# A mixture-of-experts loop: transposes moved from TensorE to VectorE, with the row layout and the weight loads that this needs

## The chip, the cores and the metric

The kernel runs on one core of one Trainium2 chip. The metric is the device time of one execution in microseconds (us), the median of three runs. Below, PE is TensorE, PEld its weight loads, DVE VectorE, ACT ScalarE, POOL GpSimd, and SP the sync engine, which here only issues DMAs. All data is float32.

## The reference

One decoder block on 512 tokens of width 1024. A gated delta-rule group and a convolution group share an input and an output projection; then each token goes to 4 of 32 experts, and a final norm follows. What matters here is the expert part:

```
xn = rmsnorm(x, ffn_norm_w)
gates, experts = softmax(top4(xn @ w_router + b_router))
for each expert e, for its tokens:
    hid = xn @ w_gate_up[e] + b_gate_up[e]            # 1024 -> 2048
    gate, up = hid[:, :1024], hid[:, 1024:]
    act = (clip(up, -7, 7) + 1) * min(gate, 7) * sigmoid(1.702 * min(gate, 7))
    y[tokens] += gates * (act @ w_down[e] + b_down[e])  # 1024 -> 1024
out = rmsnorm(x + y, final_norm_w)
```

The weights of one expert are 8 MiB (gate and up) and 4 MiB (down), read from HBM once; over 32 experts that is 403 MB. 512 tokens with 4 experts each make 2048 pairs of a token and an expert, 64 to an expert on average.

## The kernel before, in words

Up to about 430 us the kernel does the two mixer groups, the output projection, the norm and the routing. Then comes the expert loop, one visit for each expert, which takes the rest but for the last 28 us.

**Tokens.** A visit has up to four groups of 32 tokens. Groups 0 and 1 are always worked on, 2 and 3 only where an expert has more than 64 or 96 tokens; unused slots of a group are pads, which point at spare rows behind the 512 real ones. The normed rows (`xn_rows`) and the sums (`acc_rows`) lie in DRAM, seen as four quarter rows of 256 elements to a row. POOL gathers with one indirect DMA a group: partition 32j+s gets quarter j of the row of slot s, 128 pieces of 1 KB. The results go back with an indirect DMA that adds into `acc_rows`, also 128 pieces of 1 KB.

**Gathered rows to the stationary operand.** A matmul wants the contracted index on the partitions. So PE turns the gathered tile (`xt_turn`, line L1808, 8 transposes of 128x128 a visit), and ACT copies it from PSUM (`xT_copy`, L849 and L850).

**gate_up(i)** (L1836). For each of 8 chunks of 128 contracted rows (1 MiB of weights, a slot of `ring`) and each group, four matmuls, one for each quarter of the output columns; they go to the four 32-partition quarters of bank g. In float32 each stands twice in the profile. In the middle of it 16 small matmuls (L1797) work out the row numbers of a later visit.

**hid_turn and act_part.** ACT copies the four banks to SBUF (`hid_copy`, L858). PE turns them (`hid_turn`, L1904, 8 transposes for the gate half, 8 for the up half). DVE adds the bias straight from PSUM (L1410, L1417) and clamps, ACT makes the sigmoid, DVE multiplies (L1424, L1429).

**down(i-1)** (L1878). Four units of 1 MiB (`dslots`), 8 matmuls for each group and unit. ACT scales the result with the gates (L866), POOL scatters it.

**Order.** Every engine's order is written out by hand. On PE a pass of the loop is gate_up(i), xt_turn, down(i-1) units 0 and 1, hid_turn of the gate half, units 2 and 3, hid_turn of the up half. SP issues, in this order, the 8 gate_up transfers of the next visit, each once PE is done with that slot, and the 4 down transfers, each once PE is done with that unit. So weights are at most about one visit ahead. All DMAs, those of POOL too, run on the same 16 DMA engines.

Elsewhere the change touches the norm ahead of the router (`normed`, L1218, DVE; POOL then writes the rows to DRAM, L525), and the turning of the biases early in the kernel (`bias_turn`, L1485).

Of the kernel before, what the change touches and what calls it, by code (L numbers as in the profile page):

```python
# [22 lines left out]
ALU = mybir.AluOpType  # L23
ACT = mybir.ActivationFunctionType
AX_X = mybir.AxisListType.X

P = 128
# [11 lines left out]
def block_kernel(nc, x, attn_norm_w, w_in, gdn_conv_w, gdn_a_log, gdn_dt_bias, gdn_norm_w, cf_dw_w, cf_dw_b,  # L39
# [30 lines left out]
    with ExitStack() as ctx:  # L70
# [48 lines left out]
        bgu_rows = wq[0:E, 0:2 * D]  # L119
# [41 lines left out]
        def take(*dims):  # L161
# [46 lines left out]
        xT = view(wq, CAP * 8, GROUPS, 2, P)  # L208
        hid = view(wq, CAP * 16, GROUPS, 512)
        sg = view(zrows, 0, GROUPS, 2, P)  # L210
        u2 = view(zrows, CAP * 8, GROUPS, 2, P)
        g2 = view(intra, 0, GROUPS, 2, P)
        actT = view(intra, CAP * 8, GROUPS, 2, P)
# [47 lines left out]

        op_done, x2_ready, rstd2_ready, xn_ready, xn_turned, xnT_ready = (sem(n) for n in (
# [5 lines left out]
        hot_ready, idx_done, idx_ready, gathered, xt_done, xt_ready = (sem(n) for n in (  # L268
            "hot_ready", "idx_done", "idx_ready", "gathered", "xt_done", "xt_ready"))
        gu_used, hid_ready, ht_done, g2_ready, sg_ready, act_ready = (sem(n) for n in (  # L270
            "gu_used", "hid_ready", "ht_done", "g2_ready", "sg_ready", "act_ready"))
# [3 lines left out]
        half_read, router_ready, rows_known = sem("half_read"), sem("router_ready"), sem("rows_known")  # L275
# [69 lines left out]
        def _(sp):  # L345
# [37 lines left out]
            for c in range(KC):  # L383
                if c == 4:
                    sp.wait_ge(op_done, T)
                if c == 6:
                    sp.wait_ge(xn_ready, T)
                gate_up(0, c)
# [17 lines left out]
            for u in range(4):  # L406
                sp.wait_ge(gu_used, m * KC + (KC + 2 * u + 2))
                sp.dma_start(view(ring, u * SLOT, 2, D),
                             w_down[0, E - 1, 2 * u * P:(2 * u + 2) * P, :].rearrange("(c p) n -> p c n", p=P)
                             ).then_inc(slot_in[u], 16)  # L410
# [12 lines left out]
        def _(pool):  # L423
# [58 lines left out]
            nc.gpsimd.memset(ubuf[:, :, 0:PAD], 0.0).then_inc(masks_ready, 1)  # L482

# [38 lines left out]

            for t in range(T):
                pool.wait_ge(xn_ready, t + 1)
                pool.dma_start(xn_dram[t * P:(t + 1) * P, :], xn[:, t % 2, :]).then_inc(xn_out[t % 2], 16)  # L525
# [43 lines left out]
            pool.wait_ge(xt_done, 1)  # L569
# [11 lines left out]
            pool.wait_ge(xt_done, 2)  # L581
# [4 lines left out]
            with pool.Fori(1, m + 2) as i:  # L586
                pool.wait_ge(idx_ready, i + 3)
                pool.wait_ge(xt_done, i + 2)
# [23 lines left out]
        def _(act):  # L612
# [175 lines left out]

            def xnT_copy(t):
# [40 lines left out]
            lgT_copy(0)  # L830
            mixT_copy(3)
            for t in range(1, T):
                xnT_copy(t)
                if t + 1 < T:
                    lgT_copy(t)
                    top_exp(t - 1)
                    x2_rstd(t + 1)
                else:
                    top_exp(t - 1)
# [7 lines left out]
            def xT_copy(v):  # L847
                act.wait_ge(xt_done, v)
                A(xT[:, 0:2, :, :], view(bank[6], 0, 2, 2, P), ACT.Copy)  # L849
                A(xT[:, 2:4, :, :], view(bank[7], 0, 2, 2, P), ACT.Copy).then_inc(xt_ready, 1)  # L850

            xT_copy(1)
            act.wait_ge(route_ready, 1)
            m = visits_less_two(act)

            def hid_copy():
                for g in range(GROUPS):
                    A(hid[:, g, :], bank[g][:, :], ACT.Copy).then_inc(hid_ready, 1)  # L858


# [15 lines left out]
            act.wait_ge(gu_used, KC)  # L876
            hid_copy()
            xT_copy(2)
            sigmoid_gate(1)
            with act.Fori(1, m + 2) as i:  # L880
                act.wait_ge(gu_used, i * KC + KC)
                act.wait_ge(ht_done, i * 2)
                hid_copy()
                xT_copy(i + 2)
# [22 lines left out]
        def _(dve):  # L907
# [303 lines left out]
            def normed(t):  # L1211
                dve.wait_ge(rstd2_ready, t + 1)
                if t >= 2:
                    dve.wait_ge(xn_out[t % 2], 16 * (t // 2))
                if t == 0:
                    dve.wait_ge(zero_out, 32)
                    dve.wait_ge(wr_in, 48)
                V.scalar_tensor_tensor(out=xn[:, t % 2, :], in0=x2[:, t, :], scalar=rstd2[:, t:t + 1],  # L1218
                                       in1=ffnw[:, :], op0=ALU.mult, op1=ALU.mult).then_inc(xn_ready, 1)

# [48 lines left out]
            normed(0)  # L1269
            residual(1)  # L1270
            normed(1)
            route(0)
            residual(2)
            normed(2)
            route(1)
            residual(3)
            normed(3)
# [93 lines left out]
            dve.sem_inc(route_ready, 1)  # L1371
            hot(1)
# [21 lines left out]

            def act_part(e, visit, base):
# [3 lines left out]
                dve.wait_ge(ht_done, visit * 2 - 1)  # L1399

                def bias(half):
# [557 lines left out]
```

## Time and profile before

| | us |
|---|---|
| median of 3 runs | 1539.28 (1538.64 to 1543.7) |
| profiled execution | 1541.16 |
| its span | 1539.3 |
| mean granted TensorE clock | 0.952 |
| PE busy | 1381.2 (90%) |
| DVE, ACT, POOL busy | 586.4, 301.0, 363.1 |
| moved by DMA | 457.74 MB, 297 GB/s over the span |

The span is the profiled time from the first to the last instruction; the profiled execution has 1.9 us around it. Busy times of engines overlap. That PE is busy for 90% does not by itself make it the bound: what ended each wait decides, and so does how full the DMA engines are, which is a resource that no engine's row shows.

### The profile page before, as it was taken

The numbers are of one execution on the slowest core, as the hardware profiler recorded it, in microseconds if no ns is written. First come the engines' busy times: TensorE is split into PE (matmuls) and PEld (weight loads), VectorE is DVE, ScalarE is ACT, GpSimd is POOL, SyncE is SP. The second block draws the span as 40 slices with busy tenths as digits, with TensorE's granted clock in tenths as the row PEclk, the third lists the DMA queues.
The fourth block names the chain that finished last, engine by engine and source line by source line (L and its number), as shares of the span: only waits on it lengthen the run. The fifth ranks groups of instructions, "written<-read, shape, count | busy, mean of one in ns | idle before, by whom it ended". The sixth has DMA issues, their size and how long they took to land.

```text
span 1539.3 us, 33738 instructions
## 1 busy us (share of the span) xinstructions
PE 1381.2 (90%) x13162; PEld 644.5 (42%) x13163; DVE 586.4 (38%) x1328; ACT 301.0 (20%) x563; POOL 363.1 (24%) x421
## 2 busy tenths in 40 slices
PE   6997989889658999999999999989999988889982
PEld 3444555555323444434454444534334343334441
DVE  2788888643432222322223222223222233222231
ACT  3122322131201112211212111221112121112122
POOL 5001111100021222432233232323223223222232
PEclk9999999979767999999999999999999999999996
DMA  9221000400366999999999999999999999999995
GB/s 307 76 74 63 1 28 1 165 1 20 149 223 248 352 374 387 405 407 396 410 399 408 408 391 408 401 408 409 407 397 404 410 408 401 403 408 404 408 380 146
DMA packets 110260, 457.74 MB, mean 297 GB/s; under 512 B 15140, under 2 KB 36132, under 8 KB 77430
## 3 DMA queue, kind: packets, MB, share of 16 engines
q1 hardware_dynamic: 86566, 427.88, 69.5%
q0 software_dynamic: 20592, 27.68, 7.6%
q10 hardware_dynamic: 3072, 1.76, 0.4%
q8 instruction: 21, 0.34, 0.1%
q14 instruction: 9, 0.07, 0.0%
HBM read 439.05 MB, written 18.22 MB: 297 GB/s over the span
## 4 chain that ended last, share of the span: by engine, by line
PE 61%; DMA 18%; DVE 11%; SPq 4%; issue 2%; ACT 2%; POOL 0%; another core or an unknown queue 0%; ACTq 0%; DVEq 0%; POOLq 0%
PE bank L1836 28%; DMA ring<-in_w_gate_up_dram 17%; PE bank L1878 13%; PE bank L1531 5%; PE bank L1698 4%; PE bank L1904 3%; DVE dslots L978 2%; SPq L376 2%; SPq L371 2%; PE bank L1808 2%; DVE qkbuf L1002 1%; PE bank L1597 1%; PE bank L1526 1%; PE bank L1797 1%; DMA rows<-in_x_dram 1%
## 5 line engine op out<-in xcount | busy, mean ns | idle before, releaser
L1836 PE MATMUL bank<-ring,wq 128*32 128x512 f32 x5184 | 590.6, 609 | 38.6 <-DMA ring<-in_w_gate_up_dram 36.3
L1836 PEld LDWEIGHTS bank<-ring,wq 128*32 128x32 f32 x5184 | 164.2, 112 | 415.1 <-issue 414.4
L1878 PE MATMUL bank<-dslots,intra 128*32 128x256 f32 x5056 | 300.3, 381 | 3.4 <-issue 1.1
L1878 PEld LDWEIGHTS bank<-dslots,intra 128*32 128x32 f32 x5056 | 168.7, 110 | 115.3 <-issue 27.9
L858 ACT ACTIVATE wq<-bank 128x512 f32<-128x512 f32 x128 | 66.1, 603 | 630.7 <-PE bank L1836 630.7
L542 POOL DMA_INDIRECT acc_rows<-rows,idx_out x83 | 154.3, 1859 | 45.8 <-POOL idx_out L532 25.6
L1410 DVE TENSOR_TENSOR intra<-bank,small 128x256 f32<-128x256 f32 x128 | 45.3, 416 | 290.4 <-PE bank L1904 258.5
L1531 PE MATMUL bank<-hbuf,ring 128*128 128x512 f32 x320 | 147.2, 601 | 0.0
L1335 DVE TENSOR_TENSOR small<-consts,bank 128x4 f32<-128x4 f32 x34 | 5.4, 159 | 329.2 <-PE bank L1797 329.2
L532 POOL COPY idx_in<-idx 128x4 int32 (+1 forms) x34 | 6.3, 184 | 450.9 <-PE bank L1808 387.2
L537 POOL DMA_INDIRECT wq<-xn_rows,idx_in x88 | 88.0, 1000 | 45.4 <-POOL idx_in L532 27.5
L978 DVE SCALAR_TENSOR_TENSOR dslots<-dslots,small 128x512 f32<-128x512 f32 x120 | 91.8, 765 | 2.7
L1531 PEld LDWEIGHTS bank<-hbuf,ring 128*128 128x128 f32 x320 | 58.6, 194 | 59.1 <-issue 59.1
L1417 DVE TENSOR_TENSOR zrows<-bank,small 128x256 f32<-128x256 f32 x128 | 45.3, 416 | 98.6 <-PE bank L1904 97.4
L872 ACT ACTIVATE zrows<-intra 128x1024 f32<-128x1024 f32 x32 | 33.8, 1057 | 206.6 <-DVE intra L1414 206.6
L1904 PE MATMUL bank<-consts,wq 128*128 128x128 f32 x512 | 71.7, 284 | 2.7 <-DVEq L1413 1.6
L549 POOL DMA_DIRECT2D spare<-in_gdn_dt_bias_dram x93 | 69.7, 856 | 0.2 <-issue 0.2
L1904 PEld LDWEIGHTS bank<-consts,wq 128*128 128x128 f32 x512 | 56.4, 143 | 28.9 <-issue 25.5
L532 POOL COPY idx_out<-idx 128x4 int32 (+1 forms) x32 | 5.9, 184 | 238.7 <-ACT rows L866 238.7
L1698 PE MATMUL bank<-ring,dslots 128*128 128x512 f32 x128 | 59.0, 610 | 1.8 <-DVE dslots L1159 1.8
L866 ACT ACTIVATE rows<-bank,small 128x256 f32<-128x256 f32 x128 | 50.0, 473 | 51.5 <-PE bank L1878 51.5
L1808 PE MATMUL bank<-consts,wq 128*128 128x128 f32 x264 | 36.9, 284 | 10.6 <-DMA wq<-xn_rows,idx_in 9.3
(275 smaller groups left out, 1062.8 us busy)
## 6 DMA issues: line engine op xcount, KB each, us to landing
ring<-in_w_gate_up_dram SPq DMA_DIRECT2D x256, 1024.0 KB
dslots<-in_w_down_dram SPq DMA_DIRECT2D x124, 1024.0 KB
ring<-in_w_in_dram SPq DMA_DIRECT2D x12, 1024.0 KB
ring<-in_w_out_dram SPq DMA_DIRECT2D x4, 1024.0 KB
ring<-in_w_down_dram SPq DMA_DIRECT2D x4, 1024.0 KB
rows<-in_x_dram SPq DMA_DIRECT2D x4, 512.0 KB, 7.5
hbuf<-in_x_dram SPq DMA_DIRECT2D x4, 512.0 KB, 4.9
xn_rows<-convbuf POOLq DMA_DIRECT2D x4, 512.0 KB, 4.9
```

The costliest lines, as they stand in the source:

```text
L537: pool.indirect_dma_start(out=xg[:, g, :], out_offset=None, in_=xn_q, in_offset=bass.IndirectOffsetOnAxis(ap=idx_in[:, g:g + 1], axis=0), ...
L542: pool.indirect_dma_start(out=acc_q, out_offset=bass.IndirectOffsetOnAxis(ap=idx_out[:, g:g + 1], axis=0), in_=yb[:, g, :], in_offset=None ...
L549: pool.dma_start(spare[0:1, k * H:(k + 1) * H], gdn_dt_bias[0:1, :]).then_inc(done, 16)
L858: A(hid[:, g, :], bank[g][:, :], ACT.Copy).then_inc(hid_ready, 1)
L866: ins = A(yb[:, g, :], bank[4 + g // 2][:, (g % 2) * QD:(g % 2 + 1) * QD], ACT.Copy, scale=gates[:, bass.ds(stage * GROUPS + g, 1)])
L978: own.mark(V.scalar_tensor_tensor(out=cacc[:, j, :], in0=ubuf[:, j, k:k + SEQ], scalar=PT[:, j, k:k + 1], in1=cacc[:, j, :], op0=ALU.mult, ...
L1531: ins = M(bank_of(s)[:, :], unit_ap(u)[:, c, half * P:(half + 1) * P], hT[:, c, :], start=(c == 0), stop=(c == KC - 1))
L1698: ins = M(pair[half][:, :], lhs, w, start=(kc == 0), stop=(kc == KC - 1))
L1808: ins = TR(b[:, c:c + P], xg[:, g, hh * P:(hh + 1) * P], ident)
L1836: ins = M(bank[g][GROUP * j:GROUP * (j + 1), :], xT[:, g, c % 2, (c // 2) * GROUP:(c // 2 + 1) * GROUP], w[:, :, j * QD:(j + 1) * QD], sta ...
L1878: ins = M(b[GROUP * j:GROUP * (j + 1), col:col + QD], actT[:, g, c % 2, (c // 2) * GROUP:(c // 2 + 1) * GROUP], w[:, cc, j * QD:(j + 1) * QD],
L1904: ins = TR(bank[6 + g // 2][:, c:c + P], hid[:, g, half * QD + hh * P:half * QD + (hh + 1) * P], ident)
```

## The change

- The turning moves to DVE, as `transpose` of 32x32 blocks: one instruction over the gathered tile (`xt_turn`, in SBUF), four over the banks (`hid_turn`, from PSUM). PE's `xt_turn` and `hid_turn` and ACT's `xT_copy` and `hid_copy` are gone.
- A block transpose turns each 32x32 block where it stands. So the contracted index of a chunk is now in another order: chunk b has, on partition 32j+s, the row 256j+32b+s. To make the gate_up weights fit as they are stored, the rows of `xn` are written to DRAM in permuted column order. ACT scales (`xn_scale`, four instructions a tile), POOL multiplies with the norm weight (four a tile).
- The down weights must follow that order. Each unit of 1 MiB is now loaded by four transfers, one into each quarter of 32 partitions, 256 KiB each.
- The bias rows are copied into permuted order by POOL before PE turns them.
- DVE's bias additions read SBUF, not PSUM.
- Gathers and scatters get a bound, so that pads, whose numbers lie beyond the 512 real rows, are left out.
- PE's down(i-1) now follows gate_up(i) at once.

The core of the diff:

```diff
+            def quarter_rows(e, j, u):
+                return w_down[0, e].rearrange("(j b s) n -> j s b n", j=4, b=KC)[j][:, 2 * u:2 * u + 2, :]
+
             def down(i, u):
                 e = i % E
-                sp.dma_start(view(dslots, u * SLOT, 2, D),
-                             w_down[0, e, 2 * u * P:(2 * u + 2) * P, :].rearrange("(c p) n -> p c n", p=P)
-                             ).then_inc(slot_in[8 + u], 16)
+                for j in range(4):
+                    sp.dma_start(view(dslots, u * SLOT, 2, D)[GROUP * j:GROUP * (j + 1), :, :],
+                                 quarter_rows(e, j, u)).then_inc(slot_in[8 + u], 16)
...
+            pool.wait_ge(bias_in, 16)
+            for half in range(2):
+                part = slice(half * D, (half + 1) * D)
+                nc.gpsimd.tensor_copy(bgu_cols[:, part].rearrange("e (b j s) -> e b j s", b=KC, j=4),
+                                      bgu_rows[:, part].rearrange("e (j b s) -> e b j s", j=4, b=KC)
+                                      ).then_inc(bias_cols, 1)
...
             for t in range(T):
-                pool.wait_ge(xn_ready, t + 1)
+                pool.wait_ge(xn_scaled, t + 1)
+                for j in range(4):
+                    v = xn[:, t % 2, j * QD:(j + 1) * QD].rearrange("p (b s) -> p b s", b=KC)
+                    nc.gpsimd.tensor_tensor(v, v, ffnw.rearrange("p (b j s) -> p j b s", b=KC, j=4)[:, j],
+                                            ALU.mult).then_inc(xn_ready, 1)
+                pool.wait_ge(xn_ready, 4 * t + 4)
                 pool.dma_start(xn_dram[t * P:(t + 1) * P, :], xn[:, t % 2, :]).then_inc(xn_out[t % 2], 16)
...
-                                        bounds_check=None).then_inc(gathered, 16)
+                                        bounds_check=4 * SEQ - 1, oob_is_err=False).then_inc(gathered, 16)
...
-                                        in_=yb[:, g, :], in_offset=None,
-                                        compute_op=ALU.add).then_inc(scattered, 16)
+                                        in_=yb[:, g, :], in_offset=None, bounds_check=4 * SEQ - 1,
+                                        oob_is_err=False, compute_op=ALU.add).then_inc(scattered, 16)
...
+            def xn_scale(t):
+                act.wait_ge(rstd2_ready, t + 1)
+                if t >= 2:
+                    act.wait_ge(xn_out[t % 2], 16 * (t // 2))
+                for j in range(4):
+                    ins = A(xn[:, t % 2, j * QD:(j + 1) * QD].rearrange("p (b s) -> p b s", b=KC),
+                            x2[:, t, :].rearrange("p (b j s) -> p j b s", b=KC, j=4)[:, j], ACT.Copy,
+                            scale=rstd2[:, t:t + 1])
+                ins.then_inc(xn_scaled, 1)
...
+            def xt_turn(visit):
+                dve.wait_ge(gathered, visit * (16 * GROUPS))
+                V.transpose(xT.rearrange("p g n -> p (g n)"), xg.rearrange("p g n -> p (g n)")
+                            ).then_inc(xt_ready, 1)
+
...
+            def hid_turn(visit):
+                dve.wait_ge(gu_used, visit * KC)
+                for g in range(GROUPS):
+                    V.transpose(hidT[:, g, :, :].rearrange("p h n -> p (h n)"), bank[g][:, :]
+                                ).then_inc(hid_ready, 1)
...
             with pe.Fori(1, m + 2) as i:
                 pe.wait_ge(hid_ready, i * GROUPS)
+                pe.wait_ge(xt_ready, i + 1)
                 gate_up(i)
-                pe.wait_ge(idx_ready, i + 3)
-                xt_turn(i * (16 * GROUPS) + 32 * GROUPS)
                 pe.wait_ge(act_ready, i)
                 pe.wait_ge(y_ready, i)
                 tokens = tokens_left(pe, i - 1)
-                down(i - 1, tokens, (0, 1))
-                pe.wait_ge(xt_ready, i + 2)
-                hid_turn(i, 0)
-                down(i - 1, tokens, (2, 3))
-                pe.wait_ge(half_read, i * 2 + 1)
-                hid_turn(i, 1)
+                down(i - 1, tokens, range(4))
```

How instructions stand on the engines, before and now. On SP, the first of the four down units in the loop, before (an `ISA` or `REGISTER_ALU` row is a wait or an address made in a register):

```order
L403 ISA
L376 ISA
L376 DMA dslots<-in_w_down_dram 128x2x1024
L403 REGISTER_ALU
L376 ISA
L376 DMA dslots<-in_w_down_dram 128x2x1024
```

And now, the same unit and the start of the next:

```order
L407 ISA
L381 ISA
L381 DMA dslots<-in_w_down_dram 32x2x1024
L381 ISA
L381 DMA dslots<-in_w_down_dram 32x2x1024
L381 ISA
L381 DMA dslots<-in_w_down_dram 32x2x1024
L381 ISA
L381 DMA dslots<-in_w_down_dram 32x2x1024
L407 REGISTER_ALU
```

One transfer to 128 partitions has become four to 32, with the same bytes. On PE, the end of gate_up(i) and the start of down(i-1) in the loop, before:

```order
L1836 MATMUL bank<-ring,wq 32x512 x16
L1803 ISA
L1808 MATMUL bank<-consts,wq 128x128 x8
L329 ISA
L329 TENSOR_LOAD left
L329 ISA x2
L1890 ISA
L1891 COMPARE_AND_BRANCH
L1878 MATMUL bank<-dslots,intra 32x256 x8
```

And now:

```order
L1832 MATMUL bank<-ring,wq 32x512 x16
L330 ISA
L330 TENSOR_LOAD left
L330 ISA x2
L1885 ISA
L1886 COMPARE_AND_BRANCH
L1874 MATMUL bank<-dslots,intra 32x256 x8
```

The 8 transposes in between are gone, and so are the two times 8 of L1904 that stood behind units 1 and 3. On DVE, the loop's pass from the last step of the row numbers to the gate half of the activation, before:

```order
L1318 TENSOR_SCALAR small<-small 128x4
L1399 ISA
L1410 ISA
L1410 TENSOR_TENSOR intra<-bank,small 128x256 x4
L1412 REGISTER_ALU
L1414 TENSOR_SCALAR intra<-intra 128x1024
```

And now:

```order
L1314 TENSOR_SCALAR small<-small 128x4
L1398 ISA
L1400 STREAM_TRANSPOSE wq<-bank 128x512 x4
L1318 REGISTER_ALU
L1319 STREAM_TRANSPOSE wq<-wq 128x1024
L1407 REGISTER_ALU
L1413 ISA
L1413 TENSOR_TENSOR intra<-wq,small 128x256 x4
```

The five transposes stand ahead of the activation; those of the banks (L1400) free them for the next gate_up.

## Rows read from the trace of the kernel before

**Rows 1.** The page: GB/s in 40 slices of 38.5 us.
```profile
GB/s 307 76 74 63 1 28 1 165 1 20 149 223 248 352 374 387 405 407 396 410 399 408 408 391 408 401 408 409 407 397 404 410 408 401 403 408 404 408 380 146
```
**Rows 2.** Windows: busy us of engines, granted PE clock, DMA share, GB/s.
```profile
480.00:520.00 40.00, 36.68 (x346) 15.65 (x346) 10.53 (x31) 7.22 (x12) 8.08 (x10) 0.87 0.77 286
600.00:1480.00 880.00, 840.35 (x9764) 364.16 (x9760) 244.49 (x659) 152.39 (x297) 255.19 (x274) 0.99 1.03 404
926.00:936.00 10.00, 10.00 (x112) 3.09 (x100) 2.35 (x12) 0.00 (x0) 0.00 (x0) 1.00 1.04 423
```
**Rows 3.** PE's waits, 640 to 1480 us: us in total, times, longest.
```profile
PE bank L1836 <- DMA ring<-in_w_gate_up_dram: 36.3, 26, 2.7
```
**Rows 4.** DMA queues from 600 to 1480 us: packets, MB, share of 16 engines.
```profile
q1 hardware_dynamic: 59897, 337.52, 93.9%
q0 software_dynamic: 15853, 17.92, 9.2%
```
**Rows 5.** The page's groups: form and count, busy us, mean ns, idle before.
```profile
L1836 PE MATMUL bank<-ring,wq 128*32 128x512 f32 x5184 | 590.6, 609 | 38.6 <-DMA ring<-in_w_gate_up_dram 36.3
```
**Rows 6.** The chain of waits, visit 3: start us, us, what.
```profile
561.77 15.59 PE bank L1836 x144
577.35 0.49 PE bank L1797 x16
577.84 5.29 PE bank L1836 x48
583.13 1.02 PE bank L1808 x8
584.15 5.62 PE bank L1878 x96
589.77 1.02 PE bank L1904 x8
590.79 5.32 PE bank L1878 x96
```
**Rows 7.** The chain of waits, start of the loop.
```profile
434.73 2.73 DMA wq<-xn_rows,idx_in
...
441.62 8.22 PE bank L1836 x48
...
478.62 0.50 PE bank L1797 x16
...
488.20 17.39 PE bank L1836 x144
```
**Rows 8.** The chain of waits, end of the loop.
```profile
1452.86 24.76 DMA ring<-in_w_gate_up_dram
...
1501.77 9.02 PE bank L1878 x128
```
**Rows 9.** Groups, 441 to 1512 us: DVE rows that bound new operations.
```profile
L1424 DVE TENSOR_TENSOR intra<-intra,zrows 128x1024 f32<-128x1024 f32 x32 | 39.0, 1218 | 0.0
L1384 DVE TENSOR_TENSOR hbuf<-bank,hbuf 128x512 f32<-128x512 f32 x4 | 2.8, 689 | 16.6 <-PE bank L1829 16.6
```
**Rows 10.** DMA from 18 to 30 us in 40 slices of 0.3 us.
```profile
GB/s 355 335 352 355 348 341 375 478 396 160 108 203 223 295 300 304 300 294 301 296 306 300 302 307 295 319 395 382 352 430 375 362 365 362 362 335 355 348 341 358
```
**Rows 11.** DMA issues: what, KB, median us to landing.
```profile
wq<-in_b_gate_up_dram ACTq DMA_DIRECT2D x1, 256.0 KB, 5.9
intra<-in_b_down_dram ACTq DMA_DIRECT2D x1, 128.0 KB, 2.2
```
**Rows 12.** Line L376: duration ns min/median/max of SP's issue, first and last us.
```profile
L376 SPq DMA_DIRECT2D dslots<-in_w_down_dram x124: 368/449/7115, 415.8 to 1465.9; - x124
```
**Rows 13.** Timelines: start us, us, what: ahead of the loop, and the biases.
```profile
413.62 1.28 DVE L1218 SCALAR_TENSOR_TENSOR convbuf<-hbuf,small,ffnw 128x1024 f32<-128x1024 f32 x1 [1.84 <-ACT small L787]
...
55.57 1.18 PE L1485 MATMUL bank<-consts,wq 32*128 32x32 f32 x16
...
94.63 1.40 POOL L492 TENSOR_TENSOR sqbuf<-qkbuf 128x512 f32<-128x512 f32 x1 [70.60 <-DVE qkbuf L1020]
```

More of the change, by code:

```diff
@@ L830, in _ @@
             lgT_copy(0)
+            xn_scale(0)
             mixT_copy(3)
@@ L1209, in residual @@
                 dve.sem_inc(x2_ready, 1)
[L1211 to L1219, printed above, removed]
             def route(t):
@@ L1398, in act_part, with biased @@
                 c = base
-                dve.wait_ge(ht_done, visit * 2 - 1)
-                def bias(half):
-                    v = bgu[:, half * KC:(half + 1) * KC, bass.ds(e, 1)]
-                    return v.rearrange("p (j hh) o -> p hh j (o)", hh=2).to_broadcast([P, 2, 4, GROUP])
-                def four(v):
-                    return v.rearrange("p hh (j s) -> p hh j s", j=4)
-                src = [view(bank[6 + g // 2], (g % 2) * 256, 2, P) for g in range(GROUPS)]
-                for g in range(GROUPS):
-                    V.tensor_tensor(four(g2[:, g, :, :]), four(src[g]), bias(0), ALU.add).then_inc(s, 1)
+                dve.wait_ge(hid_ready, visit * GROUPS)
+                def biased(out, half):
+                    bias = bgu[:, half * KC:(half + 1) * KC, bass.ds(e, 1)]
+                    bias = bias.rearrange("p b o -> p (b o)").rearrange("p (b o) -> p b o", o=1)
+                    for g in range(GROUPS):
+                        V.tensor_tensor(out[:, g, :].rearrange("p (b s) -> p b s", b=KC),
+                                        hidT[:, g, half, :].rearrange("p (b s) -> p b s", b=KC),
+                                        bias.to_broadcast([P, KC, GROUP]), ALU.add).then_inc(s, 1)
+                biased(g2, 0)
                 c = c + GROUPS
                 dve.wait_ge(s, c)
-                dve.sem_inc(half_read, 1)
                 V.tensor_scalar(g2, g2, LIMIT, None, ALU.min).then_inc(g2_ready, 1)
-                dve.wait_ge(ht_done, visit * 2)
-                for g in range(GROUPS):
-                    V.tensor_tensor(four(u2[:, g, :, :]), four(src[g]), bias(1), ALU.add).then_inc(s, 1)
+                biased(u2, 1)
                 c = c + GROUPS
                 dve.wait_ge(s, c)
-                dve.sem_inc(half_read, 1)
                 V.tensor_scalar(u2, u2, LIMIT, -LIMIT, ALU.min, ALU.max).then_inc(s, 1)
@@ L1800, in idx_mm @@
                 ins.then_inc(idx_done, 1)
-            def xt_turn(g_wait):
-                pe.wait_ge(gathered, g_wait)
-                for g in range(GROUPS):
-                    for hh in range(2):
-                        b = bank[6 + g // 2]
-                        c = (g % 2) * 256 + hh * P
-                        ins = TR(b[:, c:c + P], xg[:, g, hh * P:(hh + 1) * P], ident)
-                ins.then_inc(xt_done, 1)
             for t in range(T):
@@ L1896, in down @@
                     down_mm(u, 1, last).then_inc(d_used, 1)
-            def hid_turn(i, half):
-                if half == 0:
-                    pe.wait_ge(hid_ready, (i + 1) * GROUPS)
-                for g in range(GROUPS):
-                    for hh in range(2):
-                        c = (g % 2) * 256 + hh * P
-                        ins = TR(bank[6 + g // 2][:, c:c + P],
-                                 hid[:, g, half * QD + hh * P:half * QD + (hh + 1) * P], ident)
-                ins.then_inc(ht_done, 1)
             pe.wait_ge(xt_ready, 1)
             gate_up(0, first=True)
-            pe.wait_ge(idx_ready, 3)
-            xt_turn(32 * GROUPS)
-            pe.wait_ge(xt_ready, 2)
-            hid_turn(0, 0)
-            pe.wait_ge(half_read, 1)
-            hid_turn(0, 1)
             with pe.Fori(1, m + 2) as i:
                 pe.wait_ge(hid_ready, i * GROUPS)
+                pe.wait_ge(xt_ready, i + 1)
                 gate_up(i)
-                pe.wait_ge(idx_ready, i + 3)
-                xt_turn(i * (16 * GROUPS) + 32 * GROUPS)
                 pe.wait_ge(act_ready, i)
```

87 lines of the change are left out of this document (37 added, 50 removed).

## The prediction

> **What bounds the kernel now.** I read the slices of the page first. From the 15th slice on (539 us) the core moves 374 to 410 GB/s and holds it to the last but one [rows 1]: a level that no longer follows the work is a resource in use. A window says how full: from 600 to 1480 us it is 404 GB/s, while a stretch without gathers or scatters shows 423 [rows 2]. So I count the weights alone. Their queue, q1, moved 337.52 MB in these 880 us, POOL's queue q0 17.92 MB [rows 4]. At 423 GB/s the weights need 337.52 / 0.423 = 798 us. The missing 82 us are what q0's traffic costs them. Nothing is left over, so from 600 us on the DMA engines are the bound.
>
> The chain of waits seems to say otherwise: in visit 3 it is nothing but PE [rows 6], and in 840 us PE waits 36.3 us for gate_up weights, 26 times and at most 2.7 us [rows 3]. Both are true. PE needs nearly as long for a visit as the DMAs do, and SP only sends for weights when PE frees a slot, so they move in step. Ahead of 600 us it is PE: from 480 to 520 us the rate is 286 GB/s [rows 2].
>
> **PE's transposes.** L1808 stands once and L1904 twice in a visit, 8 transposes and 1.02 us each time: 3.06 us [rows 6]. They go. While the DMAs bound the visit this gives nothing. It gives something in three places.
> Start: the last gather lands at 434.73 + 2.73 = 437.46, and the first matmul starts at 441.62 [rows 7], 4.2 us later. Now one DVE transpose of 128x1024 stands there. No row has one. Bounds: 1.22 us, the two-input operation of that size [rows 9], and twice that. I take 1.22 and 0.3 for semaphores: 2.6 us gained. Then from 478.62, the end of gate_up(0), to the next at 488.20 are 9.6 us [rows 7]; now PE waits there for four turns of a bank, 0.69 each by the PSUM row of that size [rows 9], 2.9 in all: 6.7 gained.
> Visits 1 to 3: each has three groups and 35.4 us on PE (561.77 to the next gate_up at 597.13: 590.79 + 5.32 + 1.02 [rows 6]). Without transposes 32.3. The DMAs need 12 x 1.048576 MB / 0.423 = 29.7 us and about 3 for the rows of three groups: 32.7. So 2.7 is gained three times, 8.
> End: from the landing of the last gate_up weights (1452.86 + 24.76 = 1477.62) to the last matmul (1501.77 + 9.02 = 1510.79) are 33.2 us [rows 8]. Now: the last four chunk-groups' matmuls 3.6, then down(30) of three groups, 10.9 [rows 6], in whose time DVE turns and activates (2.9 + 1.2 + about 8: 12), then 1 and 9.0: 25.7. Gained 7.5.
> Sum so far: 2.6 + 6.7 + 8 + 7.5 = 25 us.
>
> **Pads.** L1836 x5184 are 81 groups (8 chunks, 4 quarters, twice: 64) [rows 5], so 81 x 32 = 2592 slots for 2048 pairs: 21% are pads. Of the 82 us, 17 go if a piece left out costs nothing, none if it costs the same. I take 17, with 1 for the stretch outside the window: 18.
>
> **Without a price for the new transfers:** 1541.2 - 25 - 18 = 1498.
>
> **The down weights.** 32 visits x 4 units x 4 quarters are 512 transfers of 256 KiB to 32 partitions each, where 128 of 1 MiB to all 128 stood. A quarter is 262 KB; at 423 GB/s it takes 0.62 us. Does it at 32 partitions? One transfer before has exactly that form: the biases of gate and up, 32 partitions, 256 KB [rows 11], with other weights in flight. Slices of 0.3 us show it [rows 10]: 348 GB/s until 19.8 us, then from 20.1 to 21.9 us 478, 396, 160, 108, 203, 223, and 300 after that (small pieces of another load run by then). The first two take the load in, then the total falls to less than half and comes back when it is through. The six slices moved 1568 x 0.3 = 470 KB in 1.8 us. The stream before would have moved 626 KB, the one after 540. Lost: 156 KB or 0.45 us by the first, 70 KB or 0.23 us by the second. A third reckoning: the 208 KB that were not the load need 0.6 us at 348; 1.2 us remain for 262 KB, or 218 GB/s, half of 423: 0.58 us lost. Below, the b_down load (32 partitions, 128 KB) landed in 2.2 us on idle engines [rows 11], which shows no harm but is too short to tell: bound 0.
> Times 512: 118 us (0.23), 230 (0.45), 297 (0.58), or 0. I take 0.45, the comparison with the nearest undisturbed stream: 1498 + 230 = 1728.
>
> The Trainium skill, "SBUF — State Buffer", section "Door 1: The DMA port swizzle", says the same as a rule: partitions 0 to 31 reach 8 of 16 ports, and partitions 32 to 63 the same 8; the trace agrees, with the fall in [rows 10]. By its asymptotes for 8 ports (218 GB/s) a quarter would cost 0.58 us more, an estimate of 1795. The same page, "Can I just issue two DMAs to hit both halves?", says that transfers to the two halves one behind the other gain only 6% by it; no run here shows that.
>
> Why can four quarters in a row not make up for each other? They stand in one queue; quarters 0 and 1 come first, then 2 and 3. If what limits a quarter is shared by 0 and 1, all engines are held at once. If every quarter has its own limit, and engines drift apart by more than a quarter's time, they would overlap. That is rival C.
>
> SP issues 16 transfers for 4. An unhindered issue takes 0.37 us at least [rows 12]; 24 issues a visit are 9 us of 38: nothing.
>
> **What else moves.** For the last token tile, DVE's `normed` (1.28 us at 413.62 [rows 13]) becomes four ACT and four POOL operations; POOL's 128x512 multiply takes 1.40 [rows 13], so 0.7 each, 2.8, and ACT about 1.5: the rows are written 3 to 4 us later, at about 419, and the gather that reads them is issued after 430. ACT's 1.5 us stand ahead of the last logits, DVE's 1.28 fewer behind it: nothing within 1 us. POOL's two copies of bias rows come at 24 us, where it then idles for 70.6 us, and PE needs them at 55.57 [rows 13]: hidden, up to 30 us. The transposes in the loop, 2.8 + 1.2 us, or twice that, lie within down(i-1), 7 us for two groups to 15 for four; DVE is busy for 28% of the time (244.49 of 880 [rows 2]). What queues behind DVE's wait for the gather is the activation, needed a whole gate_up later.
>
> **Rivals.**
> A, the forecast: narrow transfers cost, 1728, own range 1600 to 1810.
> B, no loss: the fall at 20.7 us came from two queues meeting, or from 8 KB pieces beside 1 KB ones, and in one queue with 4 KB pieces the quarters run at 423 GB/s. For it: b_down. Against: gathers too mix two queues, and 404 is the worst mean they make. Time: 1498, 1485 to 1520. This is the case on the other side: it decides whether a quarter costs less than 0.08 us extra (43 us over 512).
> C, the engines drift apart, so that some fill one half while others fill the other. For it: nothing makes them keep step. Against: they get all four transfers of a unit together. At 0.15 us a quarter: 1498 + 77 = 1575, 1545 to 1600.
> D, the pads save nothing and PE's clock falls, since PE now waits: in the first visit 48 matmuls took 8.22 us [rows 7] where 5.3 is usual. A three-group visit of 32.3 us would be 50 at that, above the DMAs' 32.7 in case B. At a mean clock of 0.95 it costs a fifth of this in the longer visits only, 30 to 45 us: 1540. In case A a visit lasts 38 us, and PE has room for most of that.
>
> **How the numbers follow.** A 0.72, B 0.19, C 0.06, D 0.03. Within 0.3% (5 us) is about what can't be told from no change. Slower: A, C and half of D, 0.79. Same: 0.02. Faster: 0.19. The profiled execution was 1.9 us over the median, so 1728 becomes 1726. From 1500 to 1810 I hold nearly all of A and C and two fifths of B, 0.82; the unknown price of a quarter makes it that wide. The likeliest case's own range is 1600 to 1810.
>
> **What would show it.** A: over the loop the rate falls to about 340 GB/s, in waves: 420 while gate_up weights come, 220 to 280 while down weights do; PE busy near 70%, and its waits for gate_up and down weights grow from 36 us to some 300. If instead the rate stays over 400, B is right, and then the start, visits 1 to 3 and the end should show the 25 us. PE's first matmul should stand 1.5 us behind the gather's landing. q0 should move a fifth less. A rate below 300 GB/s would mean that something dearer than half speed is at work, such as a fixed cost of each transfer.

## The result, and the profile after

The changed kernel took 2017.8 us (median of 4 runs, 1997.9 to 2096.9), the kernel before, beside it on the same chip, 1541.5: a ratio of 1.2987 (95% interval 1.293 to 1.3044). The four runs lie 5% apart; the ratio goes by the two shortest, 1997.9 and 2005.8, mean 2001.9, and so do the differences below. The forecast was 1726 us and its range ended at 1810. The direction was right. The profiled execution took 2005.8 us, its span is 2004.1 us, the mean granted clock 0.865.

The page of the changed kernel, busy tenths and GB/s in 40 slices of 50.1 us (before: [rows 1]):

```profile
PE   7988898928997678767776766666656665666762
...
DMA  8210011067999999999999998888888788888884
GB/s 261 76 63 1 21 67 62 14 191 260 313 329 311 289 291 292 305 320 309 296 284 275 270 263 255 260 256 249 262 254 249 252 254 253 246 242 248 245 202 136
```

Two things stand in the GB/s row. From the 11th slice on (501 us) the core moves about 300 GB/s where it moved 404. And the rate falls on, to 242 in the 36th, though the weights of a visit stay the same. There the DMA row shows an 8: the engines are no longer full.

Windows of the changed kernel (columns as in [rows 2]), and PE's waits from 640 to 1900 us (as in [rows 3]):

```profile
600.00:1940.00 1340.00, 901.69 (x9060) 311.41 (x9052) 334.44 (x783) 70.84 (x135) 253.37 (x270) 0.85 0.91 269
700.00:800.00 100.00, 79.02 (x848) 28.88 (x840) 29.96 (x70) 5.25 (x10) 19.55 (x21) 0.88 1.03 293
1700.00:1800.00 100.00, 64.06 (x608) 21.09 (x600) 22.48 (x55) 5.03 (x10) 15.64 (x17) 0.81 0.81 238
```

```profile
PE bank L1832 <- DMA ring<-in_w_gate_up_dram: 293.2, 89, 7.5
PE bank L1874 <- DMA dslots<-in_w_down_dram: 117.8, 63, 3.1
```

PE waits 411 us for weights where it waited 36.3 [rows 3]. The DMA share falls from 1.03 at 700 us to 0.81 at 1700, the rate from 293 to 238 GB/s.

DMA of the changed kernel, 40 slices of 2.25 us each: first from 520 to 610 us, then from 1200 to 1290 us.

```profile
GB/s 330 197 204 242 242 231 226 290 290 261 228 393 422 415 426 422 406 402 426 286 186 272 296 257 237 229 231 220 224 273 415 402 422 422 400 373 365 375 341 224
```

```profile
DMA  4779999999999999998236565999999999999959
GB/s 107 169 231 160 306 242 293 360 384 382 390 397 373 413 284 217 204 235 187 60 107 177 138 153 124 246 164 406 390 319 386 384 390 390 384 379 317 208 122 218
```

In visits 2 and 3 the waves are as foretold: mostly 365 to 426 GB/s while gate_up weights come, 186 to 296, around half of 423, while down weights do. Some 15 visits later the gate_up part is mostly at 360 to 413. The down part starts at the half (284, 217, 204, 235) and then falls below it, mostly to 60 to 177 GB/s, with 2 to 6 tenths of the engines busy. SP's timeline shows it from the side of the issue (start, us):

```profile
581.44 25.86 SPq L381 DMA_DIRECT2D dslots<-in_w_down_dram  x16
607.98 15.88 SPq L372 DMA_DIRECT2D ring<-in_w_gate_up_dram  x8
...
651.26 16.10 SPq L372 DMA_DIRECT2D ring<-in_w_gate_up_dram  x8
...
1746.21 35.07 SPq L381 DMA_DIRECT2D dslots<-in_w_down_dram  x16
1781.96 16.48 SPq L372 DMA_DIRECT2D ring<-in_w_gate_up_dram  x8
...
1834.08 16.66 SPq L372 DMA_DIRECT2D ring<-in_w_gate_up_dram  x8
```

SP needs 35 us to put 16 down transfers into the queue where it needed 26. At 0.37 us for an unhindered issue [rows 12] it would be 6, so SP is held up in both visits; I take it that the queue is full. From one first gate_up issue to the next, a visit takes 43.3 us early (607.98 to 651.26), 49.0 at 1058 us, and from 1258 us on about 52 (1781.96 to 1834.08): it grows, and then stays. So there are two questions: what halves the rate, and what is lost beyond the half.

### The profile page after: what moved, and what is told of

It is laid out like the page before. It is cut to its first block, busy times and chain, and to the rows that moved or that the text cites. A ratio compares the mean times of both kernels' runs of the same rounds, so it can differ in the third digit from the quotient of the medians.

```text
span 2004.1 us, 33300 instructions
## 1 busy us (share of the span) xinstructions
PE 1429.1 (71%) x12386; PEld 578.8 (29%) x12387; DVE 697.1 (35%) x1485; ACT 209.0 (10%) x385; POOL 380.5 (19%) x439
## 4 chain that ended last, share of the span: by engine, by line
SPq 37%; DMA 26%; PE 22%; DVE 8%; issue 4%; ACT 2%; POOL 0%; ACTq 0%; DVEq 0%; POOLq 0%
SPq L381 24%; DMA ring<-in_w_gate_up_dram 23%; SPq L372 12%; PE bank L1832 9%; PE bank L1538 4%; PE bank L1705 3%; DVE dslots L988 2%; PE bank L1874 2%; DMA dslots<-in_w_down_dram 1%; DVE qkbuf L1012 1%; PE bank L1604 1%; PE bank L1533 1%; DMA rows<-in_x_dram 1%; PE bank L1598 1%; PE bank L1671 0%
## 5 line engine op out<-in xcount | busy, mean ns | idle before, releaser
L1832 PE MATMUL bank<-ring,wq 128*32 128x512 f32 x5184 | 708.9, 704 | 338.1 <-DMA ring<-in_w_gate_up_dram 318.1
L1874 PE MATMUL bank<-dslots,intra 128*32 128x256 f32 x5056 | 330.0, 414 | 131.4 <-DMA dslots<-in_w_down_dram 130.8
L889 ACT ACTIVATE zrows<-intra 128x1024 f32<-128x1024 f32 x32 | 33.9, 1058 | 1191.5 <-DVE intra L1420 1191.5
L558 POOL DMA_INDIRECT acc_rows<-rows,idx_out x83 | 133.5, 1608 | 48.5 <-POOL idx_out L548 26.0
L1400 DVE STREAM_TRANSPOSE wq<-bank 128x512 f32<-128x512 f32 x128 | 80.3, 685 | 175.1 <-PE bank L1832 175.1
L553 POOL DMA_INDIRECT wq<-xn_rows,idx_in x88 | 108.1, 1228 | 47.8 <-POOL idx_in L548 30.0
L1432 DVE SCALAR_TENSOR_TENSOR intra<-zrows,intra 128x1024 f32<-128x1024 f32 x32 | 39.3, 1227 | 182.8 <-PE bank L1874 182.7
L883 ACT ACTIVATE rows<-bank,small 128x256 f32<-128x256 f32 x128 | 50.1, 474 | 261.1 <-PE bank L1874 261.1
L1413 DVE TENSOR_TENSOR zrows<-wq,small 128x256 f32<-128x256 f32 x128 | 45.6, 419 | 0.0
L1413 DVE TENSOR_TENSOR intra<-wq,small 128x256 f32<-128x256 f32 x128 | 44.5, 411 | 0.0
L1310 DVE TENSOR_SCALAR rows<-slot_no,small 128x512 bf16<-128x512 bf16 x140 | 39.9, 349 | 9.9 <-DVE idx L1346 9.6
L1319 DVE STREAM_TRANSPOSE wq<-wq 128x1024 f32<-128x1024 f32 x33 | 39.8, 1205 | 5.7 <-DMA wq<-xn_rows,idx_in 5.7
```

Of the source, the lines that this page charges most:

```text
L558: pool.indirect_dma_start(out=acc_q, out_offset=bass.IndirectOffsetOnAxis(ap=idx_out[:, g:g + 1], axis=0), in_=yb[:, g, :], in_offset=None ...
L1400: V.transpose(hidT[:, g, :, :].rearrange("p h n -> p (h n)"), bank[g][:, :]).then_inc(hid_ready, 1)
L1413: V.tensor_tensor(out[:, g, :].rearrange("p (b s) -> p b s", b=KC), hidT[:, g, half, :].rearrange("p (b s) -> p b s", b=KC), bias.to_broad ...
L1832: ins = M(bank[g][GROUP * j:GROUP * (j + 1), :], xT[:, g, c * GROUP:(c + 1) * GROUP], w[:, :, j * QD:(j + 1) * QD], start=(c == 0), stop=( ...
L1874: ins = M(b[GROUP * j:GROUP * (j + 1), col:col + QD], actT[:, g, c * GROUP:(c + 1) * GROUP], w[:, cc, j * QD:(j + 1) * QD], start=(c == 0 ...
```

## The experiments

Two theories for the half. **N** (neighbours): a transfer's rate depends on which partitions it writes, and 32 neighbours get half. **F** (size or number): four transfers of 256 KB for one of 1 MB cost by themselves. A theory for what lies beyond it, **L** (lag): the 16 engines get out of step, which adds up. Times are medians; a ratio is to the kernel before, measured beside it on the same chip. Where there were only two runs and they differ by more than 1%, no ratio is given, and both are named.

### e1_wide: the same kernel with whole down transfers

gate_up's matmuls read the weight columns with a step, so that behind `hid_turn` the rows stand in the order in which the down weights and the biases are stored. `down_from` is the unit's slice of the weights as before, `part` the whole of it.

```diff
-            w = view(ring, c * SLOT, 2, D)
+            w = view(ring, c * SLOT, 2, D).rearrange("p h (b j s) -> p h j b s", b=KC, j=4)
...
-                    w[:, :, j * QD:(j + 1) * QD], start=(c == 0), stop=(c == KC - 1))
+                    w[:, :, j], start=(c == 0), stop=(c == KC - 1))
...
-                    sp.dma_start(view(dslots, u * SLOT, 2, D)[GROUP * j:GROUP * (j + 1), :, :],
-                                 quarter_rows(e, j, u)).then_inc(slot_in[8 + u], 16)
+                    sp.dma_start(view(dslots, u * SLOT, 2, D)[part], down_from(e, u)[part]).then_inc(
+                        slot_in[8 + u], 16)
```

> The changed kernel with each unit of down weights loaded by one transfer to 128 partitions again. So that the stored row order fits, gate_up reads its weight columns with a step (8 runs of 32) instead, and the biases need no permuting. All else as changed: transposes on VectorE, pads left out. Theory N (transfers to 32 neighbouring partitions run at half rate, and that is the whole loss): 1485 to 1515 us, my sum without a price for these transfers was 1498. Rival T (something else in the change costs: VectorE's transposes, the bounds on the gathers, the order of down): 1900 us or more. Between 1530 and 1900: both.

1531.4 us, ratio 0.9949 (0.9921 to 0.9978), and 1529.1 on another chip (`e14_wide_again`, 0.9928, 0.9905 to 0.9952). Everything else in the change, but for the biases' copy on POOL, is a gain of 0.5%. The whole loss, some 470 us, hangs on how the down weights are loaded. The time lies 16 us above the range that I had expected by theory N, though: the base of the forecast, 1498, was too low (see below).

### e2_quarters, e3_stride, e4_columns: four transfers for one, cut in three ways

All three are e1_wide with four transfers of 256 KB a unit (one line of each is shown, with numbers written in for names; PE's waits count the transfers accordingly):

```diff
-    DOWN_PARTS = [(slice(0, P), slice(0, 2), slice(0, D))]
+    e2: [(slice(32 * j, 32 * (j + 1)), slice(0, 2), slice(0, D)) for j in range(4)]   # 32 neighbours
+    e3: [(slice(j, P, 4), slice(0, 2), slice(0, D)) for j in range(4)]                # every fourth partition
+    e4: [(slice(0, P), slice(c, c + 1), slice(512 * h, 512 * (h + 1))) for c in range(2) for h in range(2)]
```

> As e1_wide, but each unit of down weights in four transfers to 32 neighbouring partitions, 256 KB each, in 4 KB pieces as in the changed kernel. Theory N and rival F (many small transfers cost, whatever partitions they write): within 2% of the changed kernel, 1960 to 2060 us. Rival T: no more than e1_wide plus 50 us.

> As e2_quarters, with the same number, size and pieces of transfers, but each to every fourth partition (j, j+4, ..., 124+j) instead of 32 neighbours. Theory N, that the place of the partitions decides: 1490 to 1560 us. Rival F, that number and size of transfers decide: 1960 to 2060 us.

> As e2_quarters with four transfers of 256 KB a unit, but each to all 128 partitions, one chunk and half the columns, in 2 KB pieces. Theory N: 1500 to 1570 us (smaller pieces may cost up to 1.5 us a visit). Rival F: 1960 to 2060 us or more.

2040.7 (2 runs, 2017.1 and 2064.3), 1528.4 (ratio 0.9924, 0.9894 to 0.9953) and 1541.6 us (1.0016, 0.9997 to 1.0035). The weights' queue from 700 to 1400 us (packets, MB, share of 16 engines) in e2 and then in e3:

```profile
q1 hardware_dynamic: 35819, 186.27, 87.8%
```

```profile
q1 hardware_dynamic: 52232, 271.83, 95.3%
```

e2 and e3 have the same number of transfers, of the same size, with the same 32 partitions' worth in each and the same 4-KB pieces. Only the place of the partitions differs, and it makes 512 us, or 489 by the shorter run of e2. N stands, F has fallen. Shorter pieces (2 KB in e4) cost 10 us.

### e5_halves, e8_order: would 64 partitions do, or another order?

e5 takes two transfers, to partitions 0 to 63 and 64 to 127; e8 is e2 with the order 0, 2, 1, 3.

> The form of e1_wide, but each down unit comes in two transfers of 512 KB, to partitions 0 to 63 and 64 to 127. Theory N (a transfer is limited by which partitions it writes, and 0 to 63 share the limit of 0 to 31): as slow as the quarters, 1950 to 2050 us, and the queue moves about 186 MB from 700 to 1400 us as in e2_quarters. Rival (twice the partitions, twice the room): 1531 to 1600 us, over 255 MB.

> The form of e2_quarters, but the four transfers of a unit go in the order 0, 2, 1, 3, so that neighbours in the queue lie in different halves. If one quarter's transfer and the next overlap in time on the 16 engines: 1600 to 1800 us, since each half then has its own room. If all engines work on the same quarter at the same time: 2000 to 2080 us, as e2_quarters (2041). With the theory that the stall is an engine that has fallen behind into a busy half: lower than e2_quarters, because the laggard then meets the other half, perhaps 1850.

2023.4 us (2 runs, 2005.9 to 2040.9) and 1977.0 (1947.5 to 2006.6). Twice the neighbouring partitions give nothing. To alternate the halves gives 3%, which is hardly more than the runs of one such kernel differ by; the weights' queue moved 195.08 MB from 700 to 1400 us, against 186.27 in e2 and 189.18 in the changed kernel. An overlap of the halves would have given 240 us or more, and the 1850 us that I had drawn from theory L for it was wrong too. The Trainium skill has the first as a rule ("SBUF — State Buffer", section "Door 1: The DMA port swizzle": partitions 0 to 63 reach the same 8 ports as 0 to 31), and here the trace agrees: 185.60 MB from 700 to 1400 us in e5, 186.27 in e2. On the second, the same page says under "Can I just issue two DMAs to hit both halves?" that two concurrent transfers, one to each half, gain only 6%; the 3% here agrees in size. But its sentence there, "The only way to hit all 16 ports is one transfer spanning all 128 partitions", does not hold here if it is read as wanting all 128: e3's transfers wrote 32 each, every fourth, and ran as fast as whole ones (271.83 MB against e1_wide's 272.06).

### e6_before_quarters: the loss put into the kernel before

The kernel before, with its down unit in four transfers of 32 neighbours and nothing else.

> The kernel before, with one edit: each down unit comes in four transfers of 32 neighbouring partitions. Theory N (the transfers alone are the loss): what e2_quarters lost against e1_wide, 509 us, comes here too: 2000 to 2080 us. Rival (the loss needs the changed order on PE and DVE): 1541 to 1800 us.

2015.8 us (2 runs, 1985.4 and 2046.1) against 1538.6. The one edit gives a loss of 447 to 508 us, as large as the whole one (460).

### e9_resync, e12_other: is it a lag that adds up?

Both are the changed kernel with one more wait on SP, once a visit. e9 waits for the down transfers before it sends gate_up's; e12 waits at the other boundary, before it sends the down transfers. The cut shows both edits at once; each kernel has only its own.

```diff
             with sp.Fori(2, m + 2) as i:
+                sp.wait_ge(slot_in[11], i * 64 - 64)      # e9
                 for c in range(KC):
                     sp.wait_ge(gu_used, (i - 1) * KC + c + 1)
                     gate_up(i, c)
+                sp.wait_ge(slot_in[7], i * 16 + 48)       # e12
                 for u in range(4):
```

> The changed kernel, but SP waits ahead of each visit's gate_up transfers until the last down unit of the visit before has landed, so that all 16 engines begin a visit together. Theory L (a visit grows from 43.5 us in visit 5 to 52.3 us in visit 20 because one engine falls behind, and its narrow pieces meet the others' wide ones): the visit stays at the early level plus about 2 us for the emptied queue, 45 to 47 us, and the time is 1880 to 1950 us. Rival (the growth has another cause: routing, longer visits, POOL's traffic): the wait only adds its 2 us a visit, 2060 to 2100 us.

> The changed kernel with SP's wait at the other boundary: ahead of each visit's down transfers until its last gate_up transfer has landed; narrow transfers still run into the next visit's wide ones without a wait. If the engines' drift adds up from visit to visit, any place that lines them up once a visit ends it: 1880 to 1930 us, as e9_resync (1883). If what costs is each meeting of narrow with following wide transfers: no gain, 2020 to 2080 us.

1883.0 us (ratio 1.2237, 1.2198 to 1.2277) and 1863.7 (1.2071, 1.2033 to 1.2109). A wait that was added made the kernel 119 and 138 us faster than the changed kernel's 2001.9 (on other chips), the second more than I had expected. The DMA engines in e9 and then in e12, from 1200 to 1290 us in slices of 2.25 us:

```profile
DMA  9999706999999999999999998589999999999999
GB/s 220 229 222 219 155 2 193 426 426 419 399 380 380 400 411 421 215 228 226 222 224 229 222 228 160 76 360 441 422 419 366 376 391 429 419 233 215 224 226 220
```

```profile
DMA  9999999998299999999999999999918999999999
GB/s 275 430 422 419 419 430 369 366 398 353 29 244 219 224 220 219 226 217 229 248 412 430 408 426 426 352 393 405 415 66 222 209 228 219 219 222 215 235 230 320
```

Now each visit has two clean levels, some 410 GB/s and 222 GB/s, with one short gap where the queue runs empty. 222 GB/s is the rate of 32 neighbours, about half of 423. The rate no longer falls in the course of the loop (e12's page: 284 to 315 GB/s in the slices 12 to 39). The timelines of SP, changed kernel first and then e12:

```profile
1206.18 16.04 SPq L372 DMA_DIRECT2D ring<-in_w_gate_up_dram  x8
1222.55 34.56 SPq L381 DMA_DIRECT2D dslots<-in_w_down_dram  x16
1257.78 16.46 SPq L372 DMA_DIRECT2D ring<-in_w_gate_up_dram  x8
```

```profile
1188.57 6.81 SPq L372 DMA_DIRECT2D ring<-in_w_gate_up_dram  x8
1223.39 8.03 SPq L381 DMA_DIRECT2D dslots<-in_w_down_dram  x16
1232.10 6.89 SPq L372 DMA_DIRECT2D ring<-in_w_gate_up_dram  x8
```

A visit takes 43.5 us (1188.57 to 1232.10) where it took 51.6 (1206.18 to 1257.78). So one wait a visit, at either boundary, keeps the visit at the length that it has early in the changed kernel: that is shown. It speaks for L and against a price of each passage from narrow to wide transfers: e12 leaves that passage as it was. But both waits also keep fewer transfers in the queue (SP puts the 16 in within 8.03 us, not 34.56), and no run separates the two. Against a full queue by itself: SP is held up in the changed kernel's early visits too (25.86 us for 16), and in e3, which lost nothing, it took 22.04 us for 16 (at 1221.04). What stays argued is the way the lag adds up, and why it stops at 52 us a visit. I think that an engine which is late with its narrow pieces meets the others' wide ones and falls back further, until the queue is held up for it while the others stand idle; the trace gives the mean of the 16 engines and doesn't name the late one.

### e10, e11, e7, e13: the norm and the pads

e10_norm is e1_wide with the norm back on DVE, in four instructions of 128x256 a tile that write the permuted order themselves (`perm` is a view of a row in that order). e11 has e3's transfers besides. e7 and e13 are e1_wide and e10_norm without the bounds, so that pads move again.

```diff
+                for j in range(4):
+                    V.scalar_tensor_tensor(out=xn[:, t % 2, j * QD:(j + 1) * QD].rearrange("p (b s) -> p b s", b=KC),
+                                           in0=perm(x2[:, t, :])[:, j], scalar=rstd2[:, t:t + 1],
+                                           in1=perm(ffnw[:, :])[:, j], op0=ALU.mult, op1=ALU.mult)
-                                        bounds_check=4 * SEQ - 1, oob_is_err=False   # e7, e13
+                                        bounds_check=None                            # e7, e13
```

> The form of e1_wide, but the norm of the expert rows is one step on VectorE (four instructions of 128x256 a token tile, written in permuted order), not four ACT and four POOL instructions. Theory: in e1_wide a DVE step of 0.30 us took 3.32 us beside POOL's multiplies, the rows were ready about 3 us later and the first matmul at 443.9 us; without them the first matmul comes at 440 to 441 us and the time is 3 us below e1_wide, 1528 us (ratio to before 0.993). Rival (the loop is bound by the DMA engines, which a later start only moves): same as e1_wide, ratio 0.995.

> e10_norm with each down unit in four transfers of 256 KB to every fourth partition, as in e3_stride. Theory: as e10_norm or up to 3 us below it, since down's first transfers arrive a quarter at a time; 1525 to 1529 us. Rival (four transfers for one cost SP and the queues something): above e10_norm by more than 3 us.

> e1_wide without the bounds on gathers and scatters: the pads move again, 2592 slots instead of 2048. By the forecast's price (21% of the 82 us that the other queue costs) it is 18 us slower than e1_wide; by e1_wide's trace, where the weights moved only 1% faster, 7 to 9 us slower, so about 1539, as before. Rival: no difference.

> e10_norm without the bounds on gathers and scatters, so the pads move again. The forecast priced them at 18 us, e1_wide's trace at 7 to 9. e7_pads and e1_wide, on different chips, had ratios to before of 0.994 and 0.995, which says 0. If pads are worth 7 to 9 us: slower than e15_norm_again by that. If a left-out piece costs as much as one that moves: the same within 2 us.

On one chip: e10_norm 1522.2 us (ratio 0.986, 0.9836 to 0.9883), e11 1524.3 (0.9873, 0.9852 to 0.9895; so e3's four transfers cost nothing here either), e7 1532.8 (0.9939, 0.9916 to 0.9962). On another: e14_wide_again 1529.1, e13_norm_pads 1529.4 (0.9925, 0.9904 to 0.9946), e15_norm_again 1519.2 (0.9864, 0.984 to 0.9888).

**Norm.** The timeline of e1_wide shows what it costs there (start, us):

```profile
415.21 2.77 POOL L533 TENSOR_TENSOR convbuf<-convbuf,ffnw 128x256 f32<-128x256 f32 x4 [6.23 <-ACT convbuf L805]
...
415.98 1.70 ACT L805 ACTIVATE convbuf<-hbuf,small 128x256 f32<-128x256 f32 x4
...
417.90 0.16 DVE L1233 RECIPROCAL small<-small 128x1 f32<-128x1 f32 x1 [4.46 <-ACT small L825]
...
418.36 3.32 DVE L1237 TENSOR_SCALAR kbg<-consts,small 128x32 f32<-128x32 f32 x1
418.88 2.76 POOL L533 TENSOR_TENSOR convbuf<-convbuf,ffnw 128x256 f32<-128x256 f32 x4
```

DVE sits idle for 4.46 us, because ACT does its scalings before the softmax step that the routing waits for, and then one small step takes 3.32 us, beginning while POOL issues a DMA (418.28, 0.58 us) and ending with POOL's four multiplications. The chains of waits give it the same size each time, from an ACT step ahead of the last two tiles' routing (`vbuf`) to the first expert matmul; e1_wide first, then e10_norm:

```profile
397.64 0.28 ACT vbuf L821
...
441.59 1.26 DVE wq L1314
...
443.91 2.76 PE bank L1827 x9
```

```profile
401.29 0.28 ACT vbuf L815
...
440.03 1.26 DVE wq L1323
...
442.23 4.28 PE bank L1836 x17
```

46.3 us against 40.9 (e14 and e15: 46.2 and 40.9; before: 399.15 to 441.62, 42.5). So 5.3 of the 10 us between e14 and e15 are shown. The first expert matmul itself wanders between executions of one kernel (443.9 and 450.9 us in e1_wide and e14), so it is the stretch that has to be compared. Behind it, to the end of the span, e14 and e15 differ by another 1.4 us (1081.6 and 1080.2), e1_wide and e10_norm by 2.4. Where the rest is isn't settled.

**Pads.** e13 against e15 says 10 us, e7 against e1_wide, by their ratios, nothing (0.9939 and 0.9949). The spans from the first expert matmul on say 3 to 6 (e7 1086.7, e1_wide 1080.7; e13 1082.9, e15 1080.2). So it is between 0 and 10 us, not the 17 that I took.

## Why the prediction was wrong, point by point

**The bound, and that narrow transfers cost: right.** The change made the DMA queue slower, and e6 shows that nothing else matters at this scale.

**The price of a quarter: too low, the first failing step.** I took 0.45 us from a comparison with the stream before it [rows 10] and held 0.58, the exact half, for the upper bound. Both come from the same 1.2 us for 262 KB. At the 348 GB/s of the stream before it such a load needs 0.75 us, at the loop's 423 only 0.62: I took the price against the slower stream and used it in the faster one. e9 and e12 show the half from start to end: 4.19 MB a visit at 222 GB/s are 18.9 us, at 423 they are 9.9; 9.0 us a visit or 0.56 a quarter, an estimated 287 us for 32 visits, where the sum had 230. The third reckoning of [rows 10], which solved for the transfer's own rate and got 218 GB/s, had the rate within 2%.

**Nothing beyond the half: the step that failed most.** The sum had no term for it. The changed kernel is 138 us slower than e12, which pays the same half and some pauses besides. As to the pauses, e12 less e1_wide is 332 us, less the 287: 45 us, 1.4 a visit. So what the queue loses by itself is about 183 us by this estimate (138 + 45), four fifths of what I had for the narrow transfers altogether. I had seen that the engines could drift apart, and priced it as a gain (rival C: one half filled while the other is). No run shows such a gain. What the runs show is a loss that a wait takes away, with a visit that goes from 43.3 to 52 us and a rate that goes from 293 to 238 GB/s; that a drift is behind it stays argued. Of the 276 us between 1726 and 2001.9, 183 are this term, 57 the price of the half, 33 the base (below), and 2 what I took off for the median.

**Bounds from one transfer don't bound a queue of 512.** That is why the range failed: its upper end was 297 us for the half, with 17 us of room to 1810. It would have failed without the growth too: the sum reckoned with visits of 38 us, the early ones took 43.3, and e12, where they stay at that, took 1863.7. I had asked of a rate below 300 GB/s that it mean something dearer than half speed, and it did; but it had no chance in the sum.

**The base without a price, 1498:** e1_wide had a span of 1524.6, 14.7 below before, where I had 43.
- Start, 2.6 gained: lost 2.3 instead (441.62 to 443.91), or 3.8 on the stretch above (42.5 to 46.3), which leaves out how PE's earlier work wanders. Behind the gather's landing 1.8 were gained (4.16 to 2.35); the transpose took 1.26 us, as taken (1.22). I had called ACT's and POOL's share in the norm nothing within 1 us; it cost 5.3 us on the stretch above. With the norm on DVE the stretch is 1.5 shorter than before.
- First pause, 6.7 gained: 1.7. In the changed layout it still lasts 7.9 us. Four bank turns were there, at 0.685 us each as taken, but the steps for the row numbers stand in front and the turn of the gathered tile behind, and gate_up waits for that too. Here e1_wide, from the end of the row-number matmuls at 481.2 (start, us):

```profile
481.22 0.16 DVE L1331 TENSOR_TENSOR small<-consts,bank 128x4 f32<-128x4 f32 x1 [4.49 <-PE bank L1799]
...
482.54 1.14 DVE L1305 TENSOR_SCALAR rows<-slot_no,small 128x512 bf16<-128x512 bf16 x4
483.72 0.17 DVE L1309 TENSOR_SCALAR small<-small 128x4 f32<-128x4 f32 x1
483.80 2.50 DVE L1395 STREAM_TRANSPOSE wq<-bank 128x512 f32<-128x512 f32 x4
486.22 1.20 DVE L1314 STREAM_TRANSPOSE wq<-wq 128x1024 f32<-128x1024 f32 x1
...
488.57 1.08 PE L1827 MATMUL bank<-ring,wq 128*32 128x512 f32 x4 [7.39 <-issue]
```

- Visits 1 to 3, 8 gained: 10. Visits 2, 3 and 4 start at 523.17, 555.20 and 587.33, 3.2, 6.6 and 9.8 us ahead. But the weights' queue had moved only 2.3 MB (5 us) more by 600 us, 53.78 against 51.53 since 415 us. PE's lead and the pads' gain were added in my sum; I think that both end in the same full queue: the last gate_up weights landed at 1469.26, 8.4 us earlier, where the terms ahead of the end made 35.
- Pads, 18: the weights' queue moved 1.0% more from 700 to 1400 us (272.06 MB against 269.44), 8 to 9 us over the loop, and the direct comparison gives 0 to 10. A piece that is left out seems to leave a small packet: under 512 bytes there are 9896 in that window, 7918 before and 7916 in e7. q0's MB fell by a fifth, as foretold, and its share of the engines by nearly as much, from 8.9% to 7.3%; why the weights gained less than 17 us from that isn't settled.
- End, 7.5: 6.4 (from the last gate_up landing to the end of the span 55.3, before 61.7).

**Of the signs foretold**, right were the waves (420, and 220 to 280) in the early visits, PE at 71% busy, q0's fifth. The rate over the loop was 269 GB/s, not 340, PE's waits were 411 us, not 300, and the first matmul stood 2.2 us behind the gather's landing, not 1.5.

## What to carry to other kernels

Before you cut a load into parts, ask which partitions each part writes: 32 or 64 neighbours ran at half rate, every fourth partition at full rate, with the same bytes. A price taken from one transfer was here only a lower bound for a queue full of them: give the time beyond it a term of its own, and try one wait of the issuing engine a visit, which here took some 120 to 140 us off. And when a layout must change, look for the operand that can be read with a step for nothing (here gate_up's weight columns) before the one that costs: with that, and the norm left on DVE, the change is 1.4% faster than before (e10_norm and e15_norm_again) instead of 30% slower.

## What the runs showed of the hardware

- Down transfers to 32 neighbouring partitions: 222 GB/s (e9, e12); to every fourth of 128: no slower than whole ones (271.83 MB of weights in 700 us, 272.06 with whole ones).
- A DVE step of 128x32 took 3.32 us instead of 0.30 beside four POOL multiplications of 128x256 from two SBUF operands (2.76 us). It began 0.5 us before the first of them, while POOL issued a DMA, and their ends lie within 0.1 us of each other (421.68 and 421.64). The changed kernel, e14 and e3 show the same 3.31 to 3.32 us; in e10_norm, without the multiplications, it took 0.30.
- Where a queue of narrow transfers had nothing to line it up, times of one kernel varied by 2 to 3% between two runs (e2, e5, e6, e8) and by 5% between four (the changed kernel); with one wait a visit (e9, e12) two runs differed by 0.1 to 0.2%.
- gate_up matmuls that read 8 pieces of 32 columns with a step take the usual 5.29 us for 48 (e1_wide), as before.
- Block transposes on DVE: 0.685 us for 128x512 from PSUM, 1.205 us for 128x1024 in SBUF.
